# Slots and norm of a tile run beside the next tile's mixing, tiles written out

## The reference, cut to what matters

```
x = x + concat(rwkv_out, attn_out) @ w_out
t = RMSNorm(x)
expert, gate = two-level top-k over t @ w_q against key1, key2
x = x + sum over the 128 slots of gate * gelu(down[expert] . t) * up[expert]
y = RMSNorm_final(x)
```

## Time and profile before

| | us |
|---|---|
| median of 3 runs (4369.14 to 4375.14) | 4369.31 |
| the profiled execution | 4367.83 |
| its span | 4365.9 |
| busy in the span: TensorE, VectorE, ScalarE, GpSimd | 3366.5, 2944.6, 1441.0, 1366.7 |
| bytes moved, mean rate over the span | 1410.30 MB, 323 GB/s |

### The profile page before, as it was taken

The page is one execution under the profiler, slowest core; times in us unless marked ns, Lnnn a source line. Parts: engine busy times, 40 slices in busy tenths (PEclk is TensorE's granted clock), DMA queues, the critical chain, the costliest instruction groups (busy, mean ns, idle before and its releaser), DMA issues.

```text
span 4365.9 us, 47921 instructions
## 1 busy us (share of the span) xinstructions
PE 3366.5 (77%) x13668; PEld 1870.5 (43%) x13668; DVE 2944.6 (67%) x6184; ACT 1441.0 (33%) x4151; POOL 1366.7 (31%) x1160
## 2 busy tenths in 40 slices
PE   9996837886877697869776977787778777876656
PEld 5554534452545253526352635254435434552222
DVE  1003356758876877687767877786777687769765
ACT  1001203432443335233523352335233423342222
POOL 0000002434333334334333433343334343434443
PEclk9997668898889898979897989888878898898778
DMA  4102228989899989989998999899889988999998
GB/s 189 51 37 80 81 78 337 388 360 371 326 390 369 367 329 405 352 334 363 383 359 332 366 396 363 323 370 403 350 324 364 403 342 331 380 396 347 405 420 358
DMA packets 228898, 1410.30 MB, mean 323 GB/s; under 512 B 34211, under 2 KB 40739, under 8 KB 77654
## 3 DMA queue, kind: packets, MB, share of 16 engines
q0 software_dynamic: 165888, 1208.03, 69.9%
q1 hardware_dynamic: 60102, 181.96, 11.1%
q10 hardware_dynamic: 2592, 16.66, 0.9%
HBM read 1387.39 MB, written 20.41 MB: 322 GB/s over the span
## 4 chain that ended last, share of the span: by engine, by line
PE 31%; DVE 27%; DMA 12%; issue 9%; ACT 6%; DVEq 0%; POOL 0%; ACTq 0%; POOLq 0%; SPq 0%; PEldq 0%
PE mx_ps L1435 14%; DVE ex_rows L1462 10%; DMA ex_rows<-experts,ex_expert_c 8%; PE mx_ps L1185 4%; DMA mx_fac<-w_q 2%; PE mx_ps L1168 2%; DVE mx_pqb L1285 1%; DVE mx_fac L1286 1%; DVE mx_pqb L1283 1%; DVE ex_x2c L1472 1%; PE mx_ps L978 1%; PE mx_ps L974 1%; PE mx_ps L971 1%; ACT ex_diag L1416 1%; ACT ex_coef L1409 1%
## 5 line engine op out<-in xcount | busy, mean ns | idle before, releaser
L1397 POOL DMA_INDIRECT ex_rows<-experts,ex_expert_c x1152 | 1361.9, 1182 | 2970.3 <-PE mx_ps L1435 1339.0
L1435 PE MATMUL mx_ps<-ex_rows,ex_diag 128*128 128x512 f32 x3168 | 1772.9, 707 | 638.3 <-ACT ex_diag L1416 627.9
L1462 DVE CUSTOM_DVE_ANT_0 ex_rows<-ex_rows,ex_tnc 128x1024 f32<-128x1024 f32 x1152 | 1376.4, 1222 | 277.2 <-DMA ex_rows<-experts,ex_expert_c 255.4
L1435 PEld LDWEIGHTS mx_ps<-ex_rows,ex_diag 128*128 128x128 f32 x3168 | 662.0, 222 | 1559.2 <-issue 898.6
L1406 ACT ACTIVATE ex_coef<-ex_coef 128x1 f32<-128x1 f32 x1152 | 224.9, 202 | 1510.1 <-DVE ex_coef L1462 1508.0
L1472 DVE SCALAR_TENSOR_TENSOR ex_x2c<-ex_rows,ex_coef,ex_x2c 128x1024 f32<-128x1024 f32 x360 | 462.5, 1285 | 140.2 <-ACT ex_coef L1409 139.4
L1416 ACT ACTIVATE ex_diag<-cn_ident,ex_coef 128x128 f32<-128x128 f32 x792 | 294.5, 397 | 18.5
L260 PE MATMUL psP<-pj_w_in_sb,pj_hT 128*128 128x432 f32 x768 | 279.6, 526 | 0.0
L1409 ACT ACTIVATE ex_coef<-ex_coef,ex_gate_c 128x1 f32<-128x1 f32 x1152 | 277.1, 282 | 4.7
L229 DVE TENSOR_SCALAR pj_proj_sb<-psP,pj_rstd_a 128x432 f32<-128x432 f32 x27 | 18.0, 668 | 279.2 <-PE psP L260 244.9
L1406 ACT ACT_TABLE_LOAD x137 | 175.8, 1283 | 90.3 <-issue 55.2
(11 more groups left out here) (297 smaller groups left out, 3999.8 us busy)
## 6 DMA issues: line engine op xcount, KB each, us to landing
mx_fac<-w_q SPq DMA_DIRECT2D x54, 512.0 KB, 11.0
mx_ex<-w_out SPq DMA_DIRECT2D x36, 512.0 KB, 10.7
mx_ex<-w_q SPq DMA_DIRECT2D x36, 512.0 KB, 13.3
ex_rows<-experts,ex_expert_c POOLq DMA_INDIRECT x1152, 9.2
mx_p_cur<-w_q SPq DMA_DIRECT2D x27, 512.0 KB, 13.0
mx_xs<-w_q SPq DMA_DIRECT2D x27, 512.0 KB, 13.1
proj_rows<-pj_proj_sb ACTq DMA_DIRECT2D x9, 1296.0 KB, 4.7
mx_p_cur<-proj_rows SPq DMA_DIRECT2D x9, 1296.0 KB, 8.5
```

Source lines behind the costliest of these rows:

```text
L1397: pool.indirect_dma_start(rows[:, s % RING, :], None, A["experts"], bass.IndirectOffsetOnAxis(expert_c[:, s:s + 1], 0))\
L1435: last = pe.matmul(bank(6 + c), diag[:, n % DIAGS, :], up[:, r, c * 512:(c + 1) * 512], start=n == 0, stop=n == len(ON_PE) - 1)
L1462: dve.tensor_tensor_reduce(out=down[:, r, :], in0=down[:, r, :], in1=tnc[:, :], scale=1.0, scalar=0.0, op0=ALU.mult, op1=ALU.add, accum_ou ...
```

## The change

Loops are gone: the eight tiles are written out in the instruction streams, so every wait is on a constant. Marks 72 to 75 (`END`) are new. A tile's slots are spread over marks 6 to 75: from mark 1 to 5 of tile t+1, `Turn` runs marks 72 to 76 of the experts before (`ahead`), 9 slots, and at mark 6 their `last`; only then the new experts' `first` (the four copies) and their first slots. In tile 0 of the loop marks 1 to 5 hold no slots. The final experts run with one slot to a mark (`alone`). The mixing's loads wait for the last weight block's use instead of `tile_end`; for that `mu` moves to `ex` and `k_a` to `arT`. `y_out` moves to `pqk`, its store to SP's queue between the mixing's loads and `route_sync`, and VectorE waits for the stored `y` before it first writes `pqk` (mark 9) where ScalarE waited before it wrote `ex`. `ON_VECTOR` has 42 slots.

```
-STAGES = ((7, 13, 0.3), (16, 20, 0.5), (25, 18, 0.4), (28, 6, 0.1), (38, 20, 0.3),
-          (42, 6, 0.7), (48, 9, 0.8), (59, 17, 0.0), (67, 13, 0.0), (71, 6, 0.3))
+BEGIN, END = 6, MARKS + 4
+STAGES = ((7, 3, 0.3), (16, 21, 0.5), (25, 18, 0.4), (28, 7, 0.1), (38, 22, 0.3),
+          (42, 7, 0.7), (48, 11, 0.8), (59, 16, 0.0), (67, 12, 0.0), (71, 2, 0.3),
+          (END, 9, 0.3))
...
+class Turn:
...
     def upto(self, mark):
         while self.mark < mark:
             self.mark += 1
+            if self.ahead and self.mark < BEGIN:
+                self.ahead.upto(MARKS + self.mark)
+            if self.ahead and self.mark == BEGIN:
+                self.ahead.finish()
+            self.experts.upto(self.mark)
...
-        mu = part(pqb, 0, (P_RWKV,))
-        kac = part(pqk, 0, (RW,))
+        mu = part(ex, 0, (P_RWKV,))
+        kac = part(arT, 0, (RW,))
...
             if not sample:
-                sp.wait_ge(tile_end.sem, tile_end.due(t, 0))
+                sp.wait_ge(w_used.sem, w_used.due(t, 0))
...
-            if not sample:
-                act.wait_ge(y_stored.sem, y_stored.due(t, 0))
...
+                    if not sample and dst is pqk and o == 0:
+                        dve.wait_ge(y_stored.sem, y_stored.due(t, 0))
...
-            y_out = part(ex, 0, (D,))
+            y_out = part(pqk, 0, (D,))
...
+            def store_y(sp, t):
+                sp.wait_ge(y_ready.sem, y_ready.due(t, 1))
+                sp.dma_start(A["y"][bass.ds(t * P, P), :], y_out).then_inc(y_stored.sem, 16)
...
-                with dve.Fori(0, T) as t:
-                    slots = experts_vector(dve, t)
+                ahead = None
+                for t in range(T):
+                    experts = experts_vector(dve, t)
+                    slots = Turn(ahead, experts)
                     dve.wait_ge(tile_end.sem, tile_end.due(t + 1, 0))
                     mix_vector(dve, t + 1, m, slots)
                     route_vector(dve, t + 1, slots)
                     dve.sem_inc(tile_end.sem, 1)
-                    hand_over(dve, t + 1, slots)
-                    slots.finish()
-                experts_vector(dve, T).finish()
+                    hand_over(dve, t + 1)
+                    slots.upto(MARKS)
+                    ahead = experts
+                ahead.finish()
+                experts_vector(dve, T).alone()
```

More of the change, by code:

```diff
@@ L324, in stage_tables @@
     for s in range(SLOTS):
-        mark = min(next(m for m, n in enumerate(upto) if n > s) + ADD_LAG, MARKS)
+        mark = min(next(m for m, n in enumerate(upto) if n > s) + ADD_LAG, END)
         owed += share[mark]
@@ L338, with __init__, upto @@
 class Experts:
[L345 to L348 removed]
+    def __init__(self, *work, first, last):
+        self.work, self.first, self.last, self.mark, self.done = work, first, last, BEGIN - 1, [0] * len(work)
+    def upto(self, mark, table=SLOTS_UPTO):
         while self.mark < mark:
             self.mark += 1
+            if self.mark == BEGIN:
+                self.first()
             for n, (run, lag) in enumerate(self.work):
[L352 removed]
+                end = table[max(0, min(self.mark - lag, len(table) - 1))]
                 if end > self.done[n]:
@@ L357, in finish, with alone, __init__, upto @@
     def finish(self):
-        self.upto(MARKS + ADD_LAG)
+        self.upto(END + ADD_LAG)
         assert all(n == SLOTS for n in self.done)
         self.last()
+    def alone(self):
+        table = [0] * BEGIN + list(range(1, SLOTS + 1))
+        self.upto(len(table) - 1 + ADD_LAG, table)
+        self.last()
+class Turn:
+    def __init__(self, ahead, experts):
+        self.ahead, self.experts, self.mark = ahead, experts, 0
+    def upto(self, mark):
+        while self.mark < mark:
+            self.mark += 1
+            if self.ahead and self.mark < BEGIN:
[3 more added lines that the diff above has]
+            self.experts.upto(self.mark)
+class Alone:
+    def upto(self, mark):
+        pass
 def constants(nc, ctx):
@@ L1493, in last @@
                     link.close()
-                return Experts((dots, 0), (add, ADD_LAG), last=last)
+                return Experts((dots, 0), (add, ADD_LAG), first=first, last=last)
             block = own.enter_context(nc.Block())
@@ L1519, in _ @@
             def _(pool):
-                with pool.Fori(0, T + 1) as t:
+                for t in range(T + 1):
                     experts_gpsimd(pool, t)
@@ L1525, in _ @@
                 act.sem_inc(tile_end.sem, 1)
-                with act.Fori(0, T) as t:
-                    slots = experts_scalar(act, t)
+                ahead = None
+                for t in range(T):
+                    experts = experts_scalar(act, t)
+                    slots = Turn(ahead, experts)
                     mix_scalar(act, t + 1, m, slots)
@@ L1553, in _ @@
                 pe.sem_inc(tile_end.sem, 1)
-                with pe.Fori(0, T) as t:
-                    slots = experts_tensor(pe, t)
+                ahead = None
+                for t in range(T):
+                    experts = experts_tensor(pe, t)
+                    slots = Turn(ahead, experts)
                     mix_tensor(pe, t + 1, m, slots)
@@ L1559, in _ @@
                     pe.sem_inc(tile_end.sem, 1)
-                    slots.finish()
-                experts_tensor(pe, T).finish()
+                    slots.upto(MARKS)
+                    ahead = experts
+                ahead.finish()
+                experts_tensor(pe, T).alone()
 def build(nc, A):
```

62 lines of the change are left out of this document (31 added, 31 removed).

## The result

The changed kernel takes 4416.57 us (median of 4 runs, 4410.83 to 4425.6) against 4369.23 us for the kernel before beside it (4 runs): a ratio of 1.0095, interval 1.0069 to 1.0121. It is slower by 47 us; 45 us of gain were forecast. Its profiled execution took 4410.83 us, with a span of 4409.0 against 4365.9 before.

A forecast was written before the change was run, and what follows sets the result against it. No engine was taken as full, DMA nearest (0.92 at 362 GB/s). Seven periods (-43.4), tile 0 (+3.3) and tail (-5) gave -45 us: 4369.3 to 4324 us, -1.0%; own range 4290 to 4358, with rivals 4255 to 4388.

The forecast's parts named there:

- Boundary, removed: From end of routing to the first mixing instruction: 28.9 us shrink to 6.3, a gain of 22.6 us a period.
- First marks, moved `last` and `first`, clock: Marks 1 to 5 dearer, +6.7 us; norm and copies uncovered at mark 6, +6.4; higher TensorE clock, -3.0.
- Marks 8 to 25: One dot more (1.2 us) and one TensorE add fewer (2.0) in these marks: -0.8 us a period.
- Marks 49 to 67 and loads: Two slots fewer on busy VectorE, -2.4 us; mixing loads moved to the top-k's start slow gathers, +0.5.
- The store: Store of `y` from mark 6 lands within 10.1 us, before VectorE first writes `pqk` at mark 9: nothing, bound +3.
- The crowded stretch: Marks 26 to 48 hold 47 slots instead of 41; the six more cost 9.0 us a period.
- p: Price of one added slot in marks 26 to 48: 1.5 us, ends 0 and 2.6; total change -117 + 48p.
- Tile 0: First tile, without slots in marks 1 to 5: adds saved (-7.4 us) against other costs, together +3.3.
- Tail: After the last end of routing: 348.3 us become 343 at 421 GB/s, -5; if finer slots bring nothing, +7.5.
- B: DMA pays for every slot in marks 26 to 48, 2.6 us each: +20, 4390 us; chance 0.18.
- A: Slack in marks 26 to 48 takes the six slots, p at 0 to 0.5: some 4260 us; chance 0.29.
- C: Nothing measurable, costs and gain cancel or a 362 GB/s memory ceiling holds: 4361 to 4378 us; chance 0.08.

The follow-up runs named there:

- `u_unrolled`: The kernel before with its five loops written out and nothing else changed: 4310.49 us, ratio 0.9847 to the kernel before.
- `l_late_loads`: The changed kernel with the mixing's loads waiting for the end of routing again: 4525.89 us, ratio 1.0342 to the kernel before.
- `g_short_rows`: The changed kernel with gathers of slots 84 to 96 fetching 4 KB instead of 8 KB per frame: 4318.27 us, ratio 0.9851 to the kernel before.
- `g_half_rows`: The changed kernel with gathers of slots 84 to 96 fetching rows for 64 of 128 frames: 4468.14 us, ratio 1.0206 to the kernel before.

## Why the prediction was wrong

Step by step, as the prediction has them:

- **Boundary, removed** (-22.6): right, -23.0. The stall was the loop's jump (`u_unrolled`), and a start 16.1 us later costs 16.0 (`l_late_loads`).
- **First marks, moved `last` and `first`, clock** (+6.7, +6.4, -3.0 = +10.1): right in sum, +8.6. The norm and copies take 6.5 us. The adds ahead of them grew by 2.1, 0.3 and 2.3 us where 2.5 each was taken. The clock of these marks is 0.84 for 34.5 us, against 0.73, near the 0.85 taken. From L762 to the transposes go 53.0 us in tile 7 (52 less the clock's gain was forecast; with the 12.2 us in which TensorE stands still its mean clock there is 0.77, so little of that gain came).
- **Marks 8 to 25** (-0.8): wrong, +3.0. One slot more stands there (21 for 20). The step counted its dot, and one add fewer elsewhere; in both structures the new counts make this stage longer, by 2.3 and 2.7 us. Which wait makes the difference wasn't looked into.
- **Marks 49 to 67 and loads** (-2.4, +0.5): right, -1.5.
- **The store** (0): right. It lands in 2.7 us (median) where the earlier trace rows had 9.1, and no instruction waits for it.
- **The crowded stretch** (+9.0, p = 1.5): this step failed. The stretch grew by 17.7 us, p = 2.95, above the upper end of 2.6 that the prediction gave. It let engines set the price for four fifths (1.25 us) and DMA for one fifth (2.6 us). The runs show DMA in that place for nearly the whole stretch: its engines are busy 151.6 of 155.4 us before and 168.8 of 173.1 after, at 390 GB/s in both, and changing the DMA time of 13 gathers alone changed the length with it (`g_short_rows`, 161.3 us; `g_half_rows`, 179.3). The signs were on record: a share of 1.00 at 403 GB/s, and a weight block with 12.71 us of wait on the chain. The prediction set them aside because VectorE waited for rows only 16.2 us and GpSimd waited 85.7 us for buffers. But a transfer that the chain waits for can be a weight block instead of a row, and GpSimd waits for a buffer while the other gathers and the blocks keep the DMA engines full. That p came out even above 2.6 has to do with the query products: there rows that fill q0 all the time leave the weight blocks a third of the rate, TensorE waits for each block, ScalarE, VectorE and GpSimd wait in turn, and at the end the DMA engines are half idle for 15.4 us.
- **Tile 0** (+3.3): +15.3. Of the missing 12, 5.8 are the crowded stretch's (+14.8 where 9.0 was taken) and 4.1 those of marks 8 to 25.
- **Tail** (-5): wrong, +8.6. The rate assumed was 421 GB/s; it is 397, against 391. 132 gathers are issued in it, where 131 were counted and 128 had been before. 4 x 1.05 MB at 397 GB/s are 10.6 us: the tail costs what its bytes cost, and "finer slots" brought at most 2.

The sum of what was missed: 7 x (8.7 in the crowded stretch + 3.8 in marks 8 to 25 - 1.7 in the rest) = 76; tile 0 12.0; tail 13.6; less 12.9 of variation at the start: 88, the distance from -45 to +43. By the prediction's own formula p = 2.95 gives -117 + 48 x 2.95 = +25 us, so this one term turns the sign; the other 18 of +43 are the other misses, marks 8 to 25 and the tail above all.

**The rivals.** B (slower, 4390) had the sign, the place and the mechanism: DMA has the last word in marks 26 to 48. Its price of 2.6 was near the 2.95; it lacked the idle end, and what marks 8 to 25 and the tail cost. `g_half_rows` doesn't speak against it, since there the bytes were halved and the DMA time wasn't. It had been said that B decides from p = 2.2; it did. A (slack) fell: the stretch grew by 17.7 us. C's memory limit of 362 GB/s fell too: 416 and 417 GB/s over 44.4 us in the windows above, 416 over the 29.7 us ahead of them.

**What stays open.** Why packets take nearly twice as long beside gathers of 64 rows (0.59 and 0.28 us instead of 0.32 and 0.16) was not tried further; all these rows went to partitions 0 to 63, and no other choice of 64 was run. How much of p is bytes and how much the idle end is known only roughly: the rows' 5.0 MB are some 13 of the 17.7 us. Why fewer than nine slots beside the query products make attention, boundary and top-k longer than their slots alone would is open too. The counts in the changed structure with 9 beside the query products and none of the new 12 slots ahead of mark 6 were not searched, so 4310 us is the best version found, not the best there is.

## What to carry to other kernels

Where work is spread by hand over a stream, ask of each stretch whether its DMA engines have time left, before asking which engine has. A share near 1 sets the price of an added transfer at its bytes over the rate, even when the engines seem to wait for each other and hardly for data. An average can hide this: a stretch at 0.89 was full for 44.4 us and half idle for 15.4. Then ask which transfer the chain waits for, and what each added one takes from it. Move slots and structure in separate kernels: here one edit (no loops) was worth 7.3 us a period, one (the overlap) lay between -6.7 and +1.1, and one (the counts) cost 10.8 to 18.6, and only their sum was to be seen. An early start that is paid for by moving work into places where it has no cover brings little: with the old counts 12.4 us gained at the boundary were 13.2 lost behind it.

## What the runs showed of the hardware

- Gathers of 8 KB rows and weight blocks in 4 KB rows together moved 412 to 417 GB/s with the DMA engines full (`before`, `after`), over 44.4 us in the latter.
- In 20 us at a full share the rows' queue and the blocks' queue sent about as many packets each: 735 and 826 with 8 KB rows, 876 and 1044 with 4 KB rows. Blocks of 512 KB came at one per 3.76 us in the first case while TensorE waited for them, and at one per 2.8 us in the second.
- With gathers of 64 rows of 8 KB instead of 128 beside them, packets took nearly twice as long (0.59 and 0.28 us for 8 and 4 KB, against 0.32 and 0.16): 236 GB/s at a full share, and no DMA time saved.
- A loop's jump cost VectorE 5.8 us at each tile. Written out, a period is 7.3 us shorter.
